# One hybrid decoder step: norm factor moved from a half step's input to its results, first chunks in four banks, loads by slabs, norm sums in strips

## What is computed

```python
def _rms(x, g):
    y = x * lax.rsqrt(jnp.mean(x * x, axis=-1, keepdims=True) + RMS_EPS)
    return y * g

def _half_ffn(h, g_pre, g_post, w_gate, w_up, w_down):
    u = _rms(h, g_pre)
    f = (jax.nn.silu(u @ w_gate) * (u @ w_up)) @ w_down
    return h + 0.5 * _rms(f, g_post)

h = _half_ffn(h, first half step)
q, k, v, gates = split(_rms(h, g_mix_pre) @ w_in)
m = sigmoid(gA) * (oA @ p_a) + sigmoid(gB) * (oB @ p_b)
h = h + _rms(m @ w_o, g_mix_post)
h = _half_ffn(h, second half step)
```

## Time and profile before

| | before |
|---|---|
| median of 3 runs | 1292.99 us (1292.88, 1292.99, 1298.64) |
| profiled execution, its own time | 1299.55 us |
| its span, first to last instruction | 1297.8 us |
| PE busy | 1258.3 us (97%), 10532 matmul records |
| PEld busy | 1217.2 us (94%) |
| DVE, ACT busy | 585.6 us (45%), 403.5 us (31%) |
| mean granted TensorE clock | 0.987 of full speed |
| DMA | 123.14 MB, mean 95 GB/s |

### The profile page before, as it was taken

How to read it: one execution, slowest core, us unless ns; L and a number is a source line. 1 busy time by engine, 2 the same in 40 slices (tenths; PEclk the granted TensorE clock), 3 DMA queues, 4 the chain that set the end, 5 groups by cost and what they waited for, 6 DMA issues and landing times.

```text
span 1297.8 us, 24456 instructions
## 1 busy us (share of the span) xinstructions
PE 1258.3 (97%) x10532; PEld 1217.2 (94%) x10532; DVE 585.6 (45%) x886; ACT 403.5 (31%) x660; POOL 5.2 (0%) x31
## 2 busy tenths in 40 slices
PE   6999999999999899999999999998999999999996
PEld 5999999999999899988988899997999999999995
DVE  6343443433337512545567723758543443433335
ACT  6221222212224432344445532435312222112221
POOL 0000000000000000000000000000000000000000
PEclk9999999999999899999999999999999999999998
DMA  5222222222222133302123175122122222222211
GB/s 198 66 97 97 97 80 82 97 89 90 90 90 83 63 110 123 102 34 82 52 96 132 50 250 206 66 98 66 66 97 97 72 90 97 97 89 90 90 58 67
DMA packets 30218, 123.14 MB, mean 95 GB/s; under 512 B 4442, under 2 KB 12658, under 8 KB 18418
## 3 DMA queue, kind: packets, MB, share of 16 engines
q1 hardware_dynamic: 30146, 122.09, 27.5%
HBM read 115.39 MB, written 6.67 MB: 94 GB/s over the span
## 4 chain that ended last, share of the span: by engine, by line
PE 92%; DVE 4%; ACT 2%; issue 1%; DVEq 1%; DMA 1%; SPq 0%; ACTq 0%
PE bank L1204 28%; PE bank L1205 27%; PE bank L1206 27%; PE bank L1229 1%; PE bank L1450 1%; PE bank L1396 1%; PE bank L1385 1%; PE bank L1467 1%; PE bank L1457 1%; PE bank L1358 1%; PE bank L1349 1%; DVE w_lo L869 1%; DVEq L863 1%; DVE f L910 1%; ACT w_hi L527 1%
## 5 line engine op out<-in xcount | busy, mean ns | idle before, releaser
L1204 PE MATMUL bank<-u_hi,w_hi 128*128 128x260 f32 x2144 | 618.1, 288 | 12.5 <-DVE u_lo L898 12.5
L1205 PE MATMUL bank<-u_lo,w_hi 128*128 128x260 f32 x2144 | 608.4, 284 | 0.0
L1206 PE MATMUL bank<-u_hi,w_lo 128*128 128x260 f32 x2144 | 608.2, 284 | 0.0
L1204 PEld LDWEIGHTS bank<-u_hi,w_hi 128*128 128x128 f32 x2144 | 406.9, 190 | 30.9 <-issue 28.3
L1206 PEld LDWEIGHTS bank<-u_hi,w_lo 128*128 128x128 f32 x2144 | 407.0, 190 | 0.0
L1205 PEld LDWEIGHTS bank<-u_lo,w_hi 128*128 128x128 f32 x2144 | 406.8, 190 | 0.1
L527 ACT ACTIVATE w_hi<-raw 128x2048 fp32r<-128x2048 f32 x87 | 166.2, 1910 | 314.6 <-PE bank L1206 314.5
L869 DVE TENSOR_TENSOR w_lo<-raw,w_hi 128x2048 fp32r<-128x2048 f32 x51 | 116.9, 2291 | 223.1 <-ACT w_hi L527 205.2
L1204 PE MATMUL bank<-hid_hi,w_hi 128*128 128x260 f32 x704 | 199.4, 283 | 0.0
L1205 PE MATMUL bank<-hid_lo,w_hi 128*128 128x260 f32 x704 | 199.0, 283 | 0.0
L1206 PE MATMUL bank<-hid_hi,w_lo 128*128 128x260 f32 x704 | 198.8, 282 | 0.0
(11 more groups left out here) (183 smaller groups left out, 1038.5 us busy)
## 6 DMA issues: line engine op xcount, KB each, us to landing
raw<-w_stream SPq DMA_DIRECT2D x90, 1024.0 KB, 4.9
raw<-w_stream SPq DMA_DIRECT2D x8, 768.0 KB, 4.4
h<-x_t SPq DMA_DIRECT2D x8, 260.0 KB, 5.6
y_t<-h SPq DMA_DIRECT2D x8, 260.0 KB, 2.6
slot_a<-vb_pool SPq DMA_DIRECT2D x8, 256.0 KB, 4.5
ka_t<-k_a SPq DMA_DIRECT2D x2, 520.0 KB, 3.0
kb_t<-k_b SPq DMA_DIRECT2D x2, 520.0 KB, 3.0
va_o<-v_a SPq DMA_DIRECT2D x2, 512.0 KB, 5.0
```

The source lines that it names most:

```text
L1204: pe.matmul(out_of(b), w, hi_x, start=first, stop=False)
L1205: pe.matmul(out_of(b), w, lo_x, start=False, stop=False)
L1206: return pe.matmul(out_of(b), v, hi_x, start=False, stop=last)
```

## The change

**Half steps on unscaled input.** Both half steps multiply gain x h (`u_top`, `u_low` read h), without the norm factor. The factor is applied to the results: DVE multiplies gate results with rinv (`gate`, in the loop L1149) into `sg`, ACT's silu runs in place on `sg` (`silu`), DVE multiplies `sg` with rinv once more (L1157, `first_hidden`) for the up results. So the first pair's products don't wait for the norm. The projection keeps scaled input (`u_scale`).

**First chunks in four banks.** The first pair of a stage goes through `first_part`: bank 2c + t holds chunk c, column tile t, and the order is group 0 of both chunks, then group 1 of both; inside, all w_hi x u_hi, then w_hi x u_lo, then w_lo x u_hi, at the start by half chunks. `start_up`, `to_projection` and `to_second_half` write the orders on PE, ACT and DVE.

**Loads.** gain, then slabs and half chunks in turn; ident before chunk 1's second half; group 1's slabs; bias and pages last. `ident_in` is now waited for before PE's first product.

**Sums in strips.** A group's 260 tokens are four strips of 65 (`QS`); strip s is summed with 32 columns of ones into partitions 32 s to 32 s + 31. ACT's root and DVE's reciprocal work on 65 columns. PE then widens the reciprocals to all partitions (`widen`: a column of ident, broadcast, against the 65 columns of each strip), and DVE reads the factor from PSUM, or from rinv (`rinv_copy`). Squares have up to eight buffers. ACT instead of DVE scales the outputs into f (`square_out`).

```diff
+            def load_half(n, x):
+                cols = slice(x * CH // 2, (x + 1) * CH // 2)
+                sp.dma_start(raw[:, n, cols], w_stream[n, :, cols]).then_inc((raw_first, raw_in)[x][n], 16)
+            sp.dma_start(gain[:], gains_in).then_inc(gain_in, 16)
+            load_x(0, 0)
+            load_half(0, 0)
+            load_x(0, 1)
+            load_half(0, 1)
+            load_x(0, 2)
+            load_x(0, 3)
+            load_half(1, 0)
+            sp.dma_start(ident[:], consts[:, 0:P]).then_inc(ident_in, 16)
+            load_half(1, 1)
...
         @block.tensor
             def sum_h(q, g):
                 for t in range(KD):
                     pe.wait_ge(h_sq, 16 * q + 8 * g + t + 1)
-                    pe.matmul(sum_pre[g][:, 0:TG], ones[:], sqh[t % 4], start=t == 0,
-                              stop=t == KD - 1).then_inc(h_summed, 1)
+                    for s in range(4):
+                        rows, cols = strip_of(s)
+                        mm = pe.matmul(sum_pre[g][rows, 0:QS], ones[:, 0:32], square_buffer(g, t)[:, cols],
+                                       start=t == 0, stop=t == KD - 1)
+                    mm.then_inc(h_summed, 1)
...
+            def widen(kind, n, g):
+                pe.wait_ge(rinv_made, norm_at(kind, n, g))
+                for s in range(4):
+                    one_row = ident[:, 32 * s:32 * s + 1].to_broadcast([P, P])
+                    mm = pe.matmul(sums_of(kind)[g][:, P + s * QS:P + (s + 1) * QS], one_row, root[:, g, P:P + QS],
+                                   start=True, stop=True)
+                mm.then_inc(rinv_wide, 1)
...
+            def start_up(n, r):
+                for g in range(G):
+                    for c in range(2):
+                        for half in range(2):
+                            for step in ("top", "mid", "low"):
+                                first_part(0, n, r, g, c, step, half)
+                            if (c, half) == (1, 0):
+                                widen("pre", 0, g)
+                        if c == 0:
+                            sum_h(0, g)
...
-            sum_h(0, 0)
-            sum_h(0, 1)
-            ffn_up(0, FFN1, R_FFN1)
+            pe.wait_ge(ident_in, 16)
+            start_up(FFN1, R_FFN1)
+            ffn_up(FFN1, R_FFN1)
...
         @block.vector
+            def first_hidden(q, g, r0):
+                for t in range(2):
+                    b = 2 * g + t
+                    dve.wait_ge(silu_made, 2 * UPS * q + b + 1)
+                    dve.tensor_tensor(sg[:, b, :], sg[:, b, :], rinv[:, g, :], ALU.mult)
+                    drain()
+                    dve.wait_ge(full[2 + t], r0 + g + 1)
+                    hidden(sg[:, b, :], out_of(2 + t), read[2 + t], tmp[:, t, :], hid_hi[:, t, tg(g)],
+                           hid_lo[:, t, tg(g)])
...
+                lo(n0 + 2)
+                lo(n0 + 3)
+                with dve.Fori(1, UPS) as i:
```

More of the change, by code:

```diff
@@ new lines, in h_slab_in, with square_h @@
+            def h_slab_in(q, g, t):
+                if q == 0:
+                    act.wait_ge(x_in[4 * g + t // 2], 16)
+                else:
+                    act.wait_ge(h_ready, 8 * (q - 1) + 4 * g + t // 2 + 1)
+            def square_h(q, g, tiles=range(KD)):
+                for t in tiles:
+                    if t % 2 == 0:
+                        h_slab_in(q, g, t)
+                    act.wait_ge(h_summed, 16 * q + 8 * g + (t - 5 if g and t > 5 else 0))
+                    act.activation(square_buffer(g, t), h[:, t, tg(g)], ACT.Square).then_inc(h_sq, 1)
@@ new lines, in rinv_copy, with u_top @@
+            def rinv_copy(q, g):
+                act.wait_ge(rinv_wide, norm_at("pre", q, g))
+                act.activation(rinv[:, g, :], sum_pre[g][:, P:P + TG], ACT.Copy).then_inc(rinv_in, 1)
+            def u_top(q, g, s):
+                if q == 1:
+                    act.wait_ge(hn_made, 4 * g + s + 1)
+                else:
+                    h_slab_in(q, g, 2 * s)
+                for t in (2 * s, 2 * s + 1):
+                    act.activation(u_hi[:, t, tg(g)], (f if q == 1 else h)[:, t, tg(g)], ACT.Copy,
@@ L882, in u_scale, with lo_piece @@
-            def u_scale(q, g):
-                dve.wait_ge(root_made, pre_root(q, g))
-                drain()
-                dve.reciprocal(rinv[:, g, :], root[:, g, :])
-                drain()
+            def lo_piece(n, x, count):
+                a, cols = n % 2, slice(x * CH // 2, (x + 1) * CH // 2)
+                dve.wait_ge((hi_half, hi_made)[x], count)
+                low = dve.tensor_tensor(w_lo[:, a, cols], raw[:, a, cols], w_hi[:, a, cols].bitcast(F32), ALU.subtract)
+                low.then_inc((lo_half, lo_made)[x], 1)
@@ L930, in outputs, with hidden @@
+            def hidden(gated, out, freed, x, top, low):
+                dve.tensor_tensor(x, gated, out, ALU.mult).then_inc(freed, 1)
+                drain()
+                dve.tensor_copy(top, x)
+                drain()
+                dve.tensor_tensor(low, x, top.bitcast(F32), ALU.subtract).then_inc(hid_made, 1)
             def outputs(p, n0):
-                last = DNS - 2 if p == 1 else DNS - 1
                 n = n0 + (DNS if p == 1 else DNS * KC)
-                for r in range(last):
+                for r in range(DNS - 2 if p == 1 else DNS - 1):
```

519 lines of the change are left out of this document (337 added, 182 removed).

## The result

The changed kernel takes 1305.58 us (median of 8 runs, 1303.91 to 1307.62) against 1294.33 us (8 runs, 1292.72 to 1298.94) for the kernel before: ratio 1.0085, 95% interval 1.007 to 1.010. It is slower by 0.85%. The measured time lies in the stated range of 1288 to 1309 and in the forecast's own range of 1300 to 1308. The profiled execution took 1306.62 us (span 1304.7); by the sum of the prediction it was to take 1306.0.

A forecast was written before the change was run, and what follows sets the result against it. TensorE, running almost without a break, was taken to bound the kernel; terms of +2.2, +8.3, -3.3 and -0.7 made +6.5 on the profiled 1299.55, 1306.0, less 4.1 to the median: 1302 us, own range 1300 to 1308, stated range 1288 to 1309.

The forecast's parts named there:

- start, to chunk 2: First half step's start: first product at 12.0, a 5.7 us wait for w_lo, half clock behind; chunk 2 2.2 us later.
- first junction: First half step to projection: group 1's chain, a 5.1 us wait for chunk 2 and two half-clock restarts, +8.3 us.
- second junction behind it: After the attention output: first pair, 5.3 us wait on DVE's order and restart at half clock, 39.5 against 39.2, +0.3 us.
- second half step: End of the second half step: one widening added, +1.0 us.
- tail: End of the kernel: shorter reciprocal (1.78 to 0.45), narrow sum -0.3, a widening +1.0; together -0.6 us.
- Strips and widenings: At the norms: a narrow sum costs 1.4 us against 3.5 for the wide one, a widening 1.0 us.
- Steady loops: 0.: Long loops: DVE's extra operations and later bank release stay hidden behind TensorE's products, costing 0 us.
- From the execution to the median: Whole run: the median has fewer or shorter half-clock restarts than the profiled execution, -4.1 us, from 1306.0 to 1302.
- Same time: Rival, whole run: the profile-to-median offset holds for the change and small prices lie lower, 1296 us; chance 38%.
- offset of 6.6 us: Kernel before: profiled execution 6.6 us above the median, read as four half-clock stretches at the junctions, 1.65 us each.
- Faster: Rival, three places: DVE and ACT have chunk 2 ready before the pair ends, 1286 or 1278 us; chance 11%.
- Strips one after the other: Rival, narrow sums: strips don't run side by side, 3.5 us a sum, 1315 us in total; chance 7%.

The follow-up runs named there:

- projection_early: Changed kernel, but in the projection ACT makes w_hi of chunk 2 before copying group 1's results of chunk 1: 1299.23 us, ratio 1.0028.
- before_again: The kernel before, unedited, run again over 12 runs: 1293.38 us, ratio 0.9994.
- half_steps_early: Changed kernel, but in both half steps chunk 2 is split ahead of the instructions that take the pair's last results: 1289.64 us, ratio 0.9954.
- three_edits: Changed kernel with chunk 2 split early in both half steps and the projection, and ident's wait moved to the first widening: 1278.89 us, ratio 0.9876.

## Why the prediction held, and where it missed

Term by term, in the profiled executions. A stretch of half clock is counted to the place where it stands, as in the prediction (0.096 us for each product at 0.216). For the kernel before, the prediction had chunk 2 begin at 49.3, 450.3 and 928.1; the timeline has it at 49.12, 450.11 and 927.92, and the column of the measured goes by these.

| term | predicted | measured |
|---|---|---|
| start, to chunk 2 | +2.2 | +0.4 |
| first half step | -1.1 | -0.9 |
| first junction | +8.3 | +8.3 |
| attention and its output | -3.6 | -3.9 |
| second junction behind it | +0.3 | +1.5 |
| second half step | +1.0 | +1.7 |
| tail | -0.6 | -0.3 |
| sum (of unrounded terms) | +6.5 | +6.9 |

That the sum came so close is partly luck: the start was put 1.8 us too high, and the second junction and the second half step together 1.9 too low.

*Start.* The first product was put at 12.0 and came at 12.05; the wait at the pair's end at 5.7 and was 5.34. Too high were the stretch up to it (31.3 against 42.45 - 12.05 = 30.4: the waits of 1.0 for the first root didn't come, and two narrow sums and two widenings took 2.5 and 1.6 instead of 2.8 and 2.0, while the 168 products at full clock took 20.9 instead of 20.2) and the half clock behind it (17.8 products, 1.7 us lost, instead of 2.5). With that loss counted to the start, chunk 2 began at 47.79 + 1.7 = 49.5, not 51.5.

*First junction.* From the last product of the half step (410.10) the pair ended at 448.37 + 2.07 = 450.44, 40.3 us later; the prediction had 38.5 + 1.7. The wait was 4.85 (5.1), the half clock behind it 27.7 products, 2.7 us lost (2.5). The mechanism, ACT's copies ahead of w_hi, stands in the rows of ACT and DVE above, and projection_early shows it by taking it away.

*Second junction.* The wait of 5.31 us is that predicted (5.3), and the short waits among group 1's first products came to 2.35 us (2.5; 1.99 of it for u_hi). The sum left out that these short waits, too, have half clock behind them: 13 products at 0.216 us, 1.2 us. This is the term that it put at nothing without a reason.

*Strips and widenings.* A narrow sum costs 1.04 us where it waits for nothing (predicted 1.4 with the change of shape), 65 ns a set of four against the 73 ns of the earlier trace rows. By the rule of the Trainium skill that the prediction weighed (TensorEngine Tiling (Array Packing), Instruction Overhead) it would have been, as an estimate, 1.8, with the four of a set taken one after the other; the trace's 1.04 doesn't agree. A widening costs 0.81 us (predicted 1.0). In the tail, behind idle time, its eight records last 1.97 us and not 1.00 (1294.21 against 24.47): therefore -0.3 there and not -0.6.

*Steady loops: 0.* This missed by 0.8 us in one place. From the first result read in the second half step's loop to that 75 items (1800 products) later it took 1145.98 - 930.99 = 214.99 us before, and 1152.36 - 936.60 = 215.76 us after:

```profile
936.60 0.43 DVE L1149 TENSOR_TENSOR sg<-bank,rinv 128x260 f32<-128x260 f32 x1 [2.94 <-PE bank L1398]
...
1152.36 0.43 DVE L1149 TENSOR_TENSOR sg<-bank,rinv 128x260 f32<-128x260 f32 x1 [2.44 <-PE bank L1398]
```

Without a gap in either: each product takes 0.1199 instead of 0.1194 us. The first half step's loop ran at the slower pace in both kernels (267.94 - 52.20 = 215.74 before), and at the faster one in before_again. In all 12 profiled executions of the change and its variants both loops have the slower pace; of the kernel before, three loops of four have the faster one. So the pace may belong to the change. Why is open; no experiment was made on it.

*From the execution to the median.* This is the step of the prediction that failed. "... in such a run the one behind the squares would go (1.7) and three would be short ones, 1.7 for 2.5: -4.1" put the median 4.1 us under the sum. It is 1.0 us under its profiled execution: 1305.58 against 1306.62. before_again shows that the premise was right for the kernel before, whose usual run has fewer half-clock stretches than the profiled one. It doesn't carry over: all eight runs of the change have a mean clock of 0.983 to 0.985. The written order puts three idle stretches of some five microseconds into the run, and half clock goes with them; by their mean clock all eight runs have it. The waits of the kernel before are shorter (4.3 at most), and at the junctions the clock falls behind them in some runs only. That their length makes this difference is likely, but no run tests it. So 1302 was 3.6 us low, 3.1 by this term and 0.6 by the sum, less 0.1 by rounding.

*The rivals.* "Same time" needed the offset of 6.6 us to hold for the change, and it didn't. "Faster" (the late chunk 2 is hidden, 1278 to 1286) did not come about in the change, but is what it becomes with the splits moved: half_steps_early (two of the three places) lies at 1289.6, and three_edits, which has all three and the move of ident's wait besides, at 1278.9. "Strips one after the other" is out by the 1.04 us.

## What to carry to other kernels

Where each engine works through a written order, read for every new consumer what stands ahead of what TensorE needs next: here four places in the order (three splits and a wait) turned a gain of 15 us (1294.3 to 1278.9) into a loss of 11. An instruction whose input is long there and whose output is needed soonest goes ahead of those that wait for the last results. And cost an idle stretch of TensorE with the clock behind it: the three here were 15.5 us of waiting and 6.2 us more at half clock. Short waits in a row can cost it too: 2.35 us of them had 1.2 us behind them.

## What the runs showed of the hardware

- Half clock can be worked away by spreading work that is there anyway: sums and products in turn kept the granted clock at 1.00 where the same work in two blocks gave 0.79 (windows 411 to 427).
- At the start the column of the granted clock doesn't show what the spacing shows. In the window 12.00 to 17.40 of the change it stands at 1.00, while 24 products take 5.4 us, 0.22 each:

```profile
12.00:17.40 5.40, 5.35 (x24) 5.35 (x25) 2.07 (x5) 2.88 (x8) 0.00 (x0) 1.00 1.06 389
```

- The long loops of the half steps run at one of two paces, 0.1194 or 0.1199 us a product, the same throughout a loop; the kernel before showed both in one execution.
